# A three-stage transformer step on one core: first transfers and products in another order, causal mask on GpSimd, squares between chunks

## The chip, the cores and the metric

One NeuronCore of a Trainium2 chip runs the kernel. The metric is the device time of one execution in microseconds (us); the other seven cores are not used. "TensorE" is the matrix engine (PE in the rows), "VectorE" DVE, "ScalarE" ACT, "GpSimd" POOL and "SyncE" SP.

## The reference

`x` is 256 rows of 1024 floats. Three layers follow one another, each with residual additions:

1. An even mixer (`moba_nsa_mixer`): RMS norm, one projection into queries, keys, values, gates; eight heads of block attention (with 256 positions there is one block, so plain causal attention with a relative bias) and eight heads with three branches each (compressed, selected, window), whose outputs are weighted by sigmoid gates; then an output projection and an MLP with `relu(h)^2`.
2. An odd mixer (`fox_mixer`): 16 heads of causal attention with a forget bias, then the same kind of MLP.

```
q, k, v, fz = _split(h @ w_in, ODD_SPLITS)
log_f = jax.nn.log_sigmoid((fz + b_forget).astype(jnp.float32))
cum = jnp.cumsum(log_f, axis=1).transpose(0, 2, 1)
s = (einsum('bhqd,bhkd->bhqk', qc, k) * scale + cq[..., None] - cum[:, :, None, :])
p = masked_softmax(s, key_pos[None, :] <= t[:, None])
```

3. A third layer: a gated feed-forward part, a mixer with eight dilated attention heads and four pooling groups, a second gated part, all three with norms modulated by a projection of `c`; a final norm.

All weights and results are float32.

## The kernel before, in words

**Precision and pace.** A float32 product is made of three faster ones of kind float32r: each operand x is split into a rounded part and a remainder, and `three` (L1375 to L1378) adds hi*lo, lo*hi and hi*hi in a PSUM bank. The activations are split when they are made (`a_hi` by ScalarE, `a_lo` by VectorE), the weights when they come in.

**The weight stream.** All large weights come in units of 128x2048 floats (1 MB), in the order in which they are used (`PHASES`), into a ring of four buffers `raw`. SyncE issues the transfer of unit u once TensorE has counted up `unit_used` for unit u-4 (L499 to L508). ScalarE rounds a unit or half a unit to `w_hi` (`round_half` L612, `advance` L623), VectorE subtracts (`rest_half` L937, `advance` L948) and counts up `lo_ready`, for which TensorE waits before the unit's first product. Each of these engines carries out its own list of instructions in order; all waiting is by semaphores.

**The start.** SyncE fetches the first 128 rows of `x`, unit 0 in halves, the other 128 rows, units 1 to 3 and a compression weight; ScalarE's own queue fetches `par`, the table of small constants, in two parts (L811, L812); GpSimd's queue fetches the relative table. ScalarE squares and sums the rows, VectorE makes the inverse root and scales them (`scale`), TensorE transposes them (`turn_rows`, L1457), ScalarE and VectorE split the transposed rows (`turned`, L666 and L1032). TensorE then makes a small product, `rel_rows` (L1612), of the relative table with a selection matrix, from which ScalarE copies `rrow` (L823); GpSimd stores it and reads it back spread over the partitions (`rel_band`), for the relative biases of the heads from the nq1 unit on. Then come units 0 and 1 (`v_even`, values) in eight parts, with the second half's transposes between, and units 2 and 3.

**The mixers.** `plan` lays each mixer out in ticks: a unit has 1, 2 or 4 parts, each a tick. In a tick every engine does what the tick's lists name: scores of a head (TensorE), logits with bias and row minimum (VectorE, L1090), exponential with sum (ScalarE, L751), weighting of the probabilities by the reciprocal sum (GpSimd, `scale` L536), their transposes (TensorE, `turn_probs` L1545) at least 3.8 planned us later, and the product with the values (L1563). `extras` hold what a stage has besides: in the even mixer `kcvc` writes bank 4, from which ScalarE copies the pairs of neighbouring positions (L715, L716), VectorE makes the blocks `blk`, TensorE compresses them (L1635) and goes through `hid30` (L1257), transposes of it (L1647), an exponential, `ck` and `kc` to the compressed scores.

**The forget attention.** Its 16 heads (numbers 24 to 39) take as bias the summed log gates `cum`, stored to DRAM and read back in four transfers of four heads each into `cum_row` (L576), the second to fourth paced by `unit_used`. The causal mask is added by TensorE: one more product per head (L1536) of an identity with the triangle `tri_r` into the two diagonal blocks of the score bank.

**The passages.** Between stages `norm_turn` does for each half t of the rows: residual addition (VectorE), squares with sum (ScalarE, L642), inverse root (both), scaling to `tok`, transposes, splitting. Half 0 is scaled by ScalarE (L682), half 1 by VectorE (L985). In the passage gf1 two norms are fused: VectorE also weighs the squares with a squared gain (`weigh`, L991). TensorE works on in the meantime: the last products of the old stage, then the first of the new that need only half 0 (`begin_hidden`, `begin_values`).

## Time and profile before

| | us |
|---|---|
| median of 3 runs | 1125.08 (1123.85 to 1128.44) |
| profiled execution | 1124.25 |
| its span (first to last instruction) | 1122.4 |
| TensorE busy in it | 1091.3 |
| VectorE busy | 766.7 |
| ScalarE busy | 573.5 |
| GpSimd busy | 98.4 |

The span is what the profiler sees; the time of an execution holds 1.85 us around it. "Busy" counts instructions in work, not waits. TensorE's matmuls overlap, so its busy time is no measure of its efficiency. The times of instructions count from the span's start.

### The profile page before, as it was taken

What the parts mean: (1) busy time and instruction counts of PE and PEld (TensorE: products, weight loads), DVE (VectorE), ACT (ScalarE), POOL (GpSimd) and SP (SyncE); (2) the same over time, 40 slices, a digit from 0 to 9 for tenths busy, and PEclk for the clock granted to TensorE, in tenths of its full rate; (3) what the DMA queues carried; (4) which work ended last, traced back from release to release, by engine and by line L of the source; (5) the groups of instructions that cost most, each with busy time, mean ns of one, the idle gap of its engine ahead of it and who ended that gap; (6) DMA issues with size and microseconds to landing.
All of it is one profiled execution on the core that took longest, in us unless ns stands there. A gap on an engine that the chain in (4) does not pass through costs nothing.

```text
span 1122.4 us, 17638 instructions
## 1 busy us (share of the span) xinstructions
PE 1091.3 (97%) x7206; PEld 979.1 (87%) x7206; DVE 766.7 (68%) x1195; ACT 573.5 (51%) x856; POOL 98.4 (9%) x195
## 2 busy tenths in 40 slices
PE   6999999999999999999999899999999999999997
PEld 5888779999988997899999789999978978999996
DVE  6667677878787775787766777776675766455455
ACT  6666765433356776743433653333355866333333
POOL 1022210101000121100000000101000100000000
PEclk9999999999999999999999999999999999999999
DMA  8752257778864733677778548777644434555551
GB/s 300 290 187 78 76 181 302 273 293 286 290 219 168 260 114 113 244 265 249 263 262 302 196 154 296 265 279 290 215 152 150 151 135 148 186 186 182 186 187 68
DMA packets 39520, 236.82 MB, mean 211 GB/s; under 512 B 4453, under 2 KB 4613, under 8 KB 16528
## 3 DMA queue, kind: packets, MB, share of 16 engines
q1 hardware_dynamic: 26640, 188.76, 46.4%
q0 software_dynamic: 12512, 46.26, 12.1%
q8 instruction: 57, 0.93, 0.3%
q10 hardware_dynamic: 288, 0.68, 0.2%
q14 instruction: 23, 0.19, 0.0%
HBM read 234.58 MB, written 1.10 MB: 210 GB/s over the span
## 4 chain that ended last, share of the span: by engine, by line
PE 88%; DVE 6%; ACT 3%; DMA 2%; issue 1%; SPq 0%; DVEq 0%; ACTq 0%
PE bank L1376 27%; PE bank L1377 26%; PE bank L1378 26%; DMA raw<-in_stream 2%; PE bank L1563 2%; DVE w_lo L937 1%; PE bank L1545 1%; PE bank L1534 1%; ACT w_hi L612 1%; PE bank L1457 1%; PE bank L1533 1%; DVE tok L964 1%; PE bank L1635 1%; DVE h L965 1%; PE bank L1505 0%
## 5 line engine op out<-in xcount | busy, mean ns | idle before, releaser
L1376 PE MATMUL bank<-a_lo,w_hi 128*128 128x256 f32 x1408 | 402.1, 286 | 1.0 <-ACT pair L716 1.0
L1378 PE MATMUL bank<-a_hi,w_hi 128*128 128x256 f32 x1408 | 398.3, 283 | 0.0
L1377 PE MATMUL bank<-a_hi,w_lo 128*128 128x256 f32 x1408 | 398.3, 283 | 0.0
L948 DVE TENSOR_TENSOR w_lo<-raw,w_hi 128x2048 fp32r<-128x2048 f32 x123 | 280.1, 2290 | 146.4 <-ACT w_hi L623 146.3
L623 ACT ACTIVATE w_hi<-raw 128x2048 fp32r<-128x2048 f32 x123 | 235.4, 1917 | 205.6 <-DMA raw<-in_stream 205.6
L1376 PEld LDWEIGHTS bank<-a_lo,w_hi 128*128 128x128 f32 x1408 | 269.7, 192 | 6.6 <-issue 2.6
L1377 PEld LDWEIGHTS bank<-a_hi,w_lo 128*128 128x128 f32 x1408 | 269.8, 192 | 1.8
L1378 PEld LDWEIGHTS bank<-a_hi,w_hi 128*128 128x128 f32 x1408 | 269.7, 192 | 0.0
L1376 PE MATMUL bank<-w_lo,hid_hi 128*128 128x512 f32 x432 | 169.0, 391 | 0.2 <-DVE w_lo L948 0.2
L1377 PE MATMUL bank<-w_hi,hid_lo 128*128 128x512 f32 x432 | 168.6, 390 | 0.0
L1378 PE MATMUL bank<-w_hi,hid_hi 128*128 128x512 f32 x432 | 168.1, 389 | 0.0
L937 DVE TENSOR_TENSOR w_lo<-raw,w_hi 128x1024 fp32r<-128x1024 f32 x102 | 124.5, 1238 | 32.9 <-ACT w_hi L612 32.3
L612 ACT ACTIVATE w_hi<-raw 128x1024 fp32r<-128x1024 f32 x102 | 104.8, 1053 | 29.4 <-DMA raw<-in_stream 29.2
L1378 PEld LDWEIGHTS bank<-w_hi,hid_hi 128*128 128x128 f32 x432 | 81.1, 188 | 17.2
L1376 PEld LDWEIGHTS bank<-w_lo,hid_hi 128*128 128x128 f32 x432 | 81.3, 188 | 16.3 <-issue 0.8
L1377 PEld LDWEIGHTS bank<-w_hi,hid_lo 128*128 128x128 f32 x432 | 81.3, 188 | 14.9
L1152 DVE CUSTOM_DVE_ANT_0 ada_raw<-ada_raw,silu_row 128x1024 f32<-128x1024 f32 x72 | 85.0, 1220 | 0.0
L543 POOL DMA_DIRECT2D ada_raw<-in_ada x72 | 38.1, 529 | 421.4 <-DVE modc L1152 421.4
L1376 PE MATMUL bank<-w_lo,a_hi 128*128 128x512 f32 (+1 forms) x160 | 63.3, 395 | 3.9 <-DVE a_lo L1028 3.3
L536 POOL TENSOR_SCALAR prob<-prob,wgt 128x256 f32<-128x256 f32 x96 | 43.8, 468 | 240.0 <-DVE wgt L1108 181.8
L795 ACT ACTIVATE hid_act<-bank 128x512 f32<-128x512 f32 x28 | 16.7, 596 | 90.6 <-PE bank L1378 90.6
L1378 PE MATMUL bank<-w_hi,a_hi 128*128 128x512 f32 (+1 forms) x160 | 61.7, 385 | 0.0
(203 smaller groups left out, 1159.2 us busy)
## 6 DMA issues: line engine op xcount, KB each, us to landing
raw<-in_stream SPq DMA_DIRECT2D x173, 1024.0 KB, 5.0
ada_raw<-in_ada POOLq DMA_DIRECT2D x72, 512.0 KB, 6.5
cmpw<-in_stream SPq DMA_DIRECT2D x4, 1024.0 KB, 8.2
rel_band<-rel_scratch POOLq DMA_DIRECT2D x2, 1024.0 KB, 10.3
cum_row<-cum_scratch POOLq DMA_DIRECT2D x4, 512.0 KB, 7.7
h<-in_x SPq DMA_DIRECT2D x2, 512.0 KB, 6.6
raw<-in_stream SPq DMA_DIRECT2D x2, 512.0 KB, 7.8
silu_row<-in_c_row POOLq DMA_DIRECT2D x2, 512.0 KB, 4.3
```

The lines of the kernel that those rows point to most:

```text
L536: ins = pool.tensor_scalar(p_, p_, wgt[:, 2 * i + t:2 * i + t + 1], 1.0, ALU.mult, ALU.mult)
L543: pool.dma_start(ada_raw[:, p % ADA_BUFS, :], ada[p]).then_inc(ada_landed[p % ADA_BUFS], 16)
L612: nc.scalar.activation(w_hi[:, u % RING, part_], raw[:, u % RING, part_], ACT.Copy).then_inc(hi_ready, 1)
L623: nc.scalar.activation(w_hi[:, u % RING, :], raw[:, u % RING, :], ACT.Copy).then_inc(hi_ready, 2)
L795: nc.scalar.activation(hid_act[:, j % 3, :], ps[MLP_BANKS[j % 3]][:, :], ACT.Relu).then_inc(act_feat, 1)
L937: nc.vector.tensor_tensor(w_lo[:, u % RING, part_], raw[:, u % RING, part_], w_hi[:, u % RING, part_].bitcast(F32), ALU.subtract).then_inc ...
L948: nc.vector.tensor_tensor(w_lo[:, u % RING, :], raw[:, u % RING, :], w_hi[:, u % RING, :].bitcast(F32), ALU.subtract).then_inc(lo_ready, 2)
L1152: nc.vector.tensor_tensor_reduce(part, part, silu_row[:, :], 1.0, 0.0, ALU.mult, ALU.add, modc[:, p:p + 1]).then_inc(ada_done, 1)
L1376: nc.tensor.matmul(dst, l_hi, r_lo, start=start, stop=False)
L1377: nc.tensor.matmul(dst, l_lo, r_hi, start=False, stop=False)
L1378: return nc.tensor.matmul(dst, l_hi, r_hi, start=False, stop=stop)
L1563: ins = nc.tensor.matmul(ps[ob][HD * half:HD * half + HD, c0 + block * P:c0 + T], v_cols(kind, block, heads[j][3], HD), probT[:, j % 4, lo ...
```

## The change

- **First transfers.** The second, larger part of `par` is fetched by SyncE behind unit 3 and no longer by ScalarE's queue at the start.
- **Products of zeros.** VectorE clears a tile first of all, and TensorE multiplies it 20 times by itself (`WARM`), 128x128 each in float32, before the first transposes.
- **The rel product** moves from ahead of units 0 and 1 to behind them, from bank 6 to bank 4; the transposes no longer wait for its inputs, and ScalarE copies `rrow` after it has split the second half's transposed rows, but still ahead of units 2 and 3. TensorE's wait for the copy moves to the `kcvc` unit.
- **Even mixer.** `nq0` is computed in bank 7 instead of 4, so its wait for the pairs goes to `qm0`. The transposes of `hid30` for the keys, the exponential behind them and `ck`/`kc` each come one tick later.
- **Causal mask.** TensorE's mask products, `ident_r`, `tri_r` and the semaphore for them go. GpSimd adds the triangle instead: for each of the four chunks of four heads one addition of 128x512 into a new tile `cum_early` (rows of half 0) and one into `cum_row` (half 1, diagonal block), each behind the chunk's landing and in GpSimd's own queue ahead of the weighting; VectorE waits for `masked` where it waited for the landing.
- **Passages.** In all six, ScalarE takes the squares of half 1 between the chunks of half 0 and scales half 1 too; VectorE no longer scales, and does its unit's remainder after the inverse root of half 1 instead of before.

```diff
@@ GpSimd
+            def mask(c):
+
+                pool.wait_ge(cum_landed[c], 16)
+                four = slice(4 * c, 4 * c + 4)
+                tri = pc_("tri", P).unsqueeze(1).to_broadcast([P, 4, P])
+                pool.tensor_tensor(cum_early[:, four, :], cum_row[:, four, 0:P], tri, ALU.add).then_inc(masked, 1)
+                pool.tensor_tensor(cum_row[:, four, P:T], cum_row[:, four, P:T], tri, ALU.add).then_inc(masked, 1)
...
-            for c in range(4):
+            pool.wait_ge(par_landed, 16)
+            for c in range(5):
+                if c < 4:
+                    if c > 0:
+                        pool.wait_ge(unit_used, FIRST["qk_fox"] + c - 1)
+                    pool.dma_start(cum_row[:, 4 * c:4 * c + 4, :], ...).then_inc(cum_landed[c], 16)
                 if c > 0:
-                    pool.wait_ge(unit_used, FIRST["qk_fox"] + c - 1)
-                pool.dma_start(cum_row[:, 4 * c:4 * c + 4, :], ...).then_inc(cum_landed[c], 16)
+                    mask(c - 1)
             scale(*FOX)
@@ SyncE
                 sp.dma_start(raw[:, u % RING, :], stream[u]).then_inc(raw_landed[u % RING], 16)
+                if u == RING - 1:
+                    sp.dma_start(par[:, COLS["pool_scale"]:N_COLS], cols[:, COLS["pool_scale"]:N_COLS]).then_inc(par_landed, 16)
@@ ScalarE
             def norm_turn(name, gain, shift=None):
 
-                for t in range(TT):
-                    squares(name, t)
-                    if t == 0:
-                        round_half()
-                        scale(name)
-                    turned(name, t, gain, shift)
-                    if t == 0:
-                        round_half()
+                squares(name, 0)
+                round_half()
+                scale(name, 0)
+                turned(name, 0, gain, shift, (0, 1))
+                square_half(name, 1, 0)
+                turned(name, 0, gain, shift, (2, 3))
+                square_half(name, 1, 1)
+                round_half()
+                root(name, 1)
+                scale(name, 1)
+                turned(name, 1, gain, shift)
...
-            act.dma_start(par[:, COLS["pool_scale"]:N_COLS], cols[:, COLS["pool_scale"]:N_COLS]).then_inc(par_landed, 16)
...
             squares("mix0", 1)
             round_half()
+            turned("mix0", 1, pc_("mix0", KT))
             act.wait_ge(rel_rows, 1)
-            nc.scalar.activation(rrow[:, :], ps[6][0:16, 0:REL], ACT.Copy).then_inc(rel_rows_sb, 1)
-            turned("mix0", 1, pc_("mix0", KT))
+            nc.scalar.activation(rrow[:, :], ps[4][0:16, 0:REL], ACT.Copy).then_inc(rel_rows_sb, 1)
             act.wait_ge(par_landed, 16)
             advance(FIRST["v_even"] + 4)
@@ VectorE
                 turned(name, 0, gain, shift, (2, 3))
-                rest_half()
...
                 else:
                     inverse_root(name, 1)
-                scale(name, 1)
+                rest_half()
                 turned(name, 1, gain, shift)
...
+            nc.vector.memset(probT[:, 0, 0:P], 0.0).then_inc(zeros_set, 1)
...
-            nc.vector.tensor_copy(ident_r[:, :], ident)
-            nc.vector.tensor_copy(tri_r[:, :], pc_("tri", P)).then_inc(const_ready, 1)
...
-                        dve.wait_ge(cum_landed[c], 16)
+                        dve.wait_ge(masked, 2 * c + 2)
@@ TensorE
-                if name == "mix0":
-                    pe.wait_ge(rel_rows_sb, 1)
...
-                if kind == "fox":
-                    ins = nc.tensor.matmul(bank[:, P:3 * P], ident_r[:, :], tri_r[:, :].unsqueeze(1).to_broadcast([P, 2, P]),
-                                           start=False, stop=True)
...
+            pe.wait_ge(zeros_set, 1)
+            for _n in range(WARM):
+                nc.tensor.matmul(ps[0][:, 0:P], probT[:, 0, 0:P], probT[:, 0, 0:P], start=True, stop=True)
+            pe.wait_ge(norms_landed, 16)
+            turn_rows("mix0", 0)
+            begin_values("mix0", lambda j, part: value_part("mix0", "v_even", j, part, 4, V1W))
             pe.wait_ge(pick_landed, 32)
             pe.wait_ge(pool_step, 1)
-            pe.wait_ge(norms_landed, 16)
-            turn_rows("mix0", 0)
-            nc.tensor.matmul(ps[6][0:16, 0:REL], relt[:, :], rpick[:, :], start=True, stop=True).then_inc(rel_rows, 1)
-            begin_values("mix0", lambda j, part: value_part("mix0", "v_even", j, part, 4, V1W))
+            nc.tensor.matmul(ps[4][0:16, 0:REL], relt[:, :], rpick[:, :], start=True, stop=True).then_inc(rel_rows, 1)
             pe.wait_ge(par_landed, 16)
...
-                for v, where in enumerate((("nq1", 0, 3), ("km0", 0, 1))):
+                for v, where in enumerate((("qm0", 0, 0), ("km0", 0, 1))):
...
-                if tick.at("qm0", 0, 2):
+                if tick.at("qm0", 0, 3):
...
                 elif tag == "kcvc":
+                    if part == 0:
+                        pe.wait_ge(rel_rows_sb, 1)
                     feature_part(u, 4, part, 2)
...
-                    if tag == "nq0" and part == 0:
+                    if tag == "qm0" and part == 0:
                         pe.wait_ge(pairs_taken, 2)
```

## Rows read from the trace of the kernel before

**Rows 1.** The page, busy time and share of the span of each engine.
```profile
PE 1091.3 (97%) x7206; PEld 979.1 (87%) x7206; DVE 766.7 (68%) x1195; ACT 573.5 (51%) x856; POOL 98.4 (9%) x195
```

**Rows 2.** TensorE's waits: us in total, times, longest.
```profile
PE bank L1457 <- DMA rpick<-in_rel_pick: 8.9, 1, 8.9
PE bank L1457 <- DVE tok L985: 5.8, 6, 2.5
PE bank L1376 <- ACT pair L716: 1.0, 1, 1.0
PE bank L1647 <- DVE hid L1257: 0.9, 1, 0.9
```

**Rows 3.** TensorE in order of time: start, us, what, idle before.
```profile
10.81 1.89 PE L1612 MATMUL bank<-rpick,relt 33*16 33x511 f32 x2
12.92 0.79 PE L1376 MATMUL bank<-w_lo,a_hi 128*128 128x512 f32 x1 [0.23 <-DVE a_lo L1032]
17.05 0.50 PE L1376 MATMUL bank<-w_lo,a_hi 128*128 128x512 f32 x1
18.22 1.04 PE L1457 MATMUL bank<-par,tok 128*128 128x128 f32 x8
19.50 0.50 PE L1376 MATMUL bank<-w_lo,a_hi 128*128 128x512 f32 x1 [0.24 <-DVE w_lo L937]
25.16 0.47 PE L1376 MATMUL bank<-w_lo,a_hi 128*128 128x512 f32 x1
```

**Rows 4.** ScalarE in order of time, the start.
```profile
10.03 1.06 ACT L612 ACTIVATE w_hi<-raw 128x1024 fp32r<-128x1024 f32 x1 [0.45 <-DMA raw<-in_stream]
17.41 0.57 ACT L823 ACTIVATE rrow<-bank 16x511 f32<-16x511 f32 x1
20.65 3.77 ACT L623 ACTIVATE w_hi<-raw 128x2048 fp32r<-128x2048 f32 x2
```

**Rows 5.** VectorE in order of time, the start.
```profile
11.12 1.22 DVE L937 TENSOR_TENSOR w_lo<-raw,w_hi 128x1024 fp32r<-128x1024 f32 x1 [0.28 <-ACT w_hi L612]
22.72 4.49 DVE L948 TENSOR_TENSOR w_lo<-raw,w_hi 128x2048 fp32r<-128x2048 f32 x2 [0.94 <-ACT w_hi L623]
```

**Rows 6.** The chain of waits, at two places: start, us, what.
```profile
654.51 1.78 PE bank L1505 x16
378.32 0.17 PE bank L1536
385.38 0.33 PE bank L1545 x3
```

**Rows 7.** GpSimd: one line, landings of cum_row, and its order of time.
```profile
L583 POOL TENSOR_TENSOR gate_row<-row x1: 2522/2522/2522, 467.0 to 467.0; 128x1024 f32<-128x1024 f32 x1
DMA to landing us min/median/max: 7.1/7.7/8.7
363.45 1.06 POOL L576 DMA_DIRECT2D cum_row<-cum_scratch  x2 [1.85 <-DMA cum_scratch<-cum]
375.32 0.53 POOL L576 DMA_DIRECT2D cum_row<-cum_scratch  x1 [5.23 <-PE bank L1378]
382.01 0.83 POOL L536 TENSOR_SCALAR prob<-prob,wgt 128x256 f32<-128x256 f32 x2 [6.17 <-DVE wgt L1108]
386.53 1.87 POOL L536 TENSOR_SCALAR prob<-prob,wgt 128x256 f32<-128x256 f32 x2 [3.69 <-DVE wgt L1108]
```

**Rows 8.** DMA issues of the first 60 us: KB, us to landing.
```profile
par<-in_cols ACTq DMA_DIRECT2D x1, 567.0 KB, 7.9
```

**Rows 9.** One stretch: busy us of engines, granted clock, DMA share, GB/s.
```profile
10.00:15.00 5.00, 4.77 (x13) 2.39 (x12) 4.25 (x11) 4.32 (x11) 0.00 (x0) 1.00 1.03 425
```

**Rows 10.** The scaling of rows on VectorE and ScalarE: ns min/median/max.
```profile
L985 DVE TENSOR_SCALAR tok<-h,stat x14: 478/483/489, 7.6 to 928.9; 128x512 f32<-128x512 f32 x14
L682 ACT ACTIVATE tok<-h,stat x10: 707/716/725, 150.7 to 920.2; 128x512 f32<-128x512 f32 x10
```

**Rows 11.** TensorE in order of time, passage gf1.
```profile
646.25 1.09 PE L1457 MATMUL bank<-par,tok 128*128 128x128 f32 x8 [2.51 <-DVE tok L985]
```

More of the change, by code:

```diff
@@ L45 @@
 ADA_BUFS = 3
+WARM = 20
 PHASES = [
@@ L239, in build @@
         cum_row = place("cum_row", [P, 16, T], at=bias_at)
+        cum_early = place("cum_early", [P, 16, P], at=V_at + 2 * D * 4)
         dil_b = place("dil_b", [P, HEADS, T], at=bias_at)
@@ L258, in build @@
         par = place("par", [P, N_COLS])
-        ident_r = place("ident_r", [P, P], F32R)
-        tri_r = place("tri_r", [P, P], F32R)
         kc = place("kc", [P, 2, 2, 16], F32R)
@@ L624, in advance, with square_half @@
                     halves[0] += 2
+            def square_half(name, t, k):
+                n = NORMS.index(name)
+                if name == "mix0":
+                    act.wait_ge(x_landed[t], 16)
+                else:
+                    act.wait_ge(h_ready, 4 * (n - 1) + 2 * t + k + 1)
+                half = slice(512 * k, 512 * k + 512)
+                accum = fin[:, t, k:k + 1] if name == "gf1" else stat[:, k, t:t + 1]
+                nc.scalar.activation(tok[:, t, half], h[:, t, half], ACT.Square, scale=1.0 / 32, accum_out=accum).then_inc(sumsq, 1)
             def squares(name, t):
-                sums_of_squares(name, t)
-                root(name, t)
-            def sums_of_squares(name, t):
-                n = NORMS.index(name)
                 if t == 0:
                     nc.scalar.activation(stat[:, 10, :], stat[:, 9, :], ACT.Sqrt)
-                for k in range(2):
-                    if name == "mix0":
-                        act.wait_ge(x_landed[t], 16)
-                    else:
-                        act.wait_ge(h_ready, 4 * (n - 1) + 2 * t + k + 1)
-                    half = slice(512 * k, 512 * k + 512)
-                    accum = fin[:, t, k:k + 1] if name == "gf1" else stat[:, k, t:t + 1]
-                    nc.scalar.activation(tok[:, t, half], h[:, t, half], ACT.Square, scale=1.0 / 32, accum_out=accum).then_inc(sumsq, 1)
+                square_half(name, t, 0)
+                square_half(name, t, 1)
+                root(name, t)
             def root(name, t):
@@ L649, in root, with turned @@
                     nc.scalar.activation(fin[:, t, 10:12], fin[:, t, 4:6], ACT.Sqrt).then_inc(root_ready, 1)
-            def turned(name, t, gain, shift=None):
+            def turned(name, t, gain, shift=None, chunks=(0, 1, 2, 3)):
                 m = TURN[name] + 4 * t
                 ts = slice(t * P, (t + 1) * P)
-                for c in range(4):
+                for c in chunks:
                     if shift is not None and c % 2:
@@ L840, in even_extras @@
                         nc.scalar.activation(hid_e[:, v, :], ps[(2, 7)[v]][HD:HD + 30, 0:256], ACT.Copy).then_inc(hidden_half, 1)
-                for v, where in enumerate((("qm0", 0, 0), ("km0", 0, 2))):
+                for v, where in enumerate((("qm0", 0, 1), ("km0", 0, 2))):
                     if tick.at(*where):
@@ L1257, in even_extras @@
                         nc.vector.tensor_tensor(hid30[:, v, :], ps[(2, 7)[v]][0:30, 0:256], hid_e[:, v, :], ALU.add).then_inc(hidden_rows, 1)
-                for v, where in enumerate((("qm0", 0, 0), ("km0", 0, 2))):
+                for v, where in enumerate((("qm0", 0, 1), ("km0", 0, 2))):
                     if tick.at(*where):
@@ L1628, in compress @@
             def compress(v, half):
+                if v == 1:
+                    pe.wait_ge(feat_taken, 2 * STACK_NO[("nq0", 0)] + 2)
                 pe.wait_ge(blocks_ready, v + 1)
```

34 lines of the change are left out of this document (16 added, 18 removed).

## The prediction

> **What bounds the kernel now.** I read the busy times first: TensorE is busy for 1091.3 of the 1122.4 us of the span [rows 1], so only what shortens TensorE's own work, or its idle 31 us, can move the end. Next come TensorE's waits [rows 2]: 8.9 us at the start for the last small transfer, 5.8 us in six passages between stages, where the second half's transposes wait for VectorE's scaled rows, 1.0 us for ScalarE's pair copies and 0.9 us for VectorE's hid30. Then I read the start in order of time on TensorE, ScalarE and VectorE [rows 3 to 5] and the stretch of the forget attention [rows 6, 7]. The profiled execution took 1124.25 us, 1.85 us more than its span, and 0.83 us less than the median of 1125.08. I add up against 1124.25 and put the 0.83 back at the end. About 0.5% (5.6 us) is what a measurement can tell here from no change.
>
> **First transfers.** The 567 KB of `par` leave the ScalarE queue, where they moved beside the first units for 7.9 us [rows 8], and go behind unit 3 on SyncE's. The transfers ran at 425 GB/s in that stretch with all the engines' share used [rows 9], so 567 KB less ahead is 1.3 to 1.6 us. Who gets it: ScalarE's second rounding at 10.03 waited for its transfer [rows 4], VectorE's remainder at 11.12 waited for ScalarE [rows 5], and TensorE's first product at 12.92 for VectorE [rows 3]. The same chain sets the product at 19.50, which waited for w_lo. Bounds: 0 (the small queue was served in gaps) to 1.6; I take 1.4, since 567 KB lie fully ahead of unit 1. SyncE issues one more transfer (0.4 us) while it has nothing due, and the compression weights behind it are used only some units later.
>
> **Zeros ahead.** 20 products of 128x128 start at about 0.9 us. Eight of the same form take 1.78 us [rows 6], 0.22 each, so twice that at half speed: they end between 5.3 and 9.8 us; the first transposes stood at 8.9 [rows 2]. What they buy is the clock. The 12 products from 12.92 take 4.13 us; the 6 after them 1.17 (17.05 to 18.22) [rows 3]. By these spacings the first ran at 1.2 GHz and the next at 2.4 GHz, although the table's granted clock says 1.00 [rows 9]. But the time saved, 1.8 us, lies ahead of waits that others set: product 19.50 waits for w_lo, whose chain runs through transfers, ScalarE and VectorE. So it is worth 0; bounds 0 to -0.3, and +0.5 if all zeros run slow.
>
> **The rel product.** Before, this product (1.89 us, at half speed) ran at 10.81 and ended when TensorE had to wait anyway; its copy by ScalarE (0.57) ran at 17.41, before ScalarE rounded units 2 and 3 (3.77 for both, at 20.65); VectorE's remainders (4.49 for both) began at 22.72, and unit 2's products at 25.16 just met them [rows 3 to 5]. Now the product stands behind the eight parts of units 0 and 1, and ScalarE waits for it before the copy and before any rounding of unit 2. Behind that wait are queued the copy, unit 2's rounding, then on VectorE its remainder, and TensorE waits for that. From the end of unit 1's products: product at full speed 0.95, semaphore and drain 0.2, copy 0.57, rounding 1.92, remainder 2.25, two hand-overs 0.1: 6.0 us, where the gap was 0.2. Unit 2 starts 5.8 later and, with the 1.4 from the transfers, 4.4 later: at 29.5 instead of 25.16. **Term: +4.4**, bounds +4.2 (transfers give 1.6) to +5.8 (they give nothing). TensorE stands idle for 5.0 of it.
>
> **What the mixer gives back.** The 1.0 us wait for the pairs [rows 2] came from ScalarE, held up by a late transfer; the compression behind it waited 0.2 us more for blk, made of the same pairs. With TensorE 4.4 us later and the first product of the nq0 unit moved to bank 7, neither is left: -1.2. hid30's transposes move one tick later (a quarter of a unit; units 2 and 3 are the stretch from 25.16 on, some 4.4 us each), more than the 0.85 us that was waited: -0.85. The chain behind them (exponential, keys, `kc`) keeps one tick of slack less; I cost that at 0, and at +1 if VectorE's `kc` is late at km0. Bounds of the two: 0 to -3.5 (all the waits of this stage). **Term: -2.05.**
>
> **Mask on GpSimd.** 16 products `tri_r x ident_r` go, each 0.17 us of the chain [rows 6]: -2.7 (bounds -2.2 to -2.7). GpSimd gets 8 additions of 128x512. The nearest row, its product of 128x1024, took 2.52 [rows 7]: 1.26 each, 2.5 per chunk. These masks stand in one queue with the transfers and with the weighting of the probabilities. In order: transfer 0, issued at 363.45, lands 7.7 later, about 371.2; mask 0 to 373.7; only then is transfer 2 issued, mask 1 to 376.8; then transfer 3 is issued (was 375.32) and lands at 384.5; mask 3 to 387.0; then head 24's weighting (0.8, before at 382.01) to 387.9. Its transposes stood at 385.38 [rows 6], 384.9 without the three mask products ahead of it. That is a new wait of 3.0 us. One more thing: at 386.53 two weightings took 1.87, at 382.01 two had taken 0.83; VectorE was subtracting two SBUF tiles meanwhile [rows 7]. Half of such a block gives 0.5 more. **Term: -2.7 + 3.5 = +0.8**, bounds -1.2 (landing 7.1 each, additions at 1.0) to +8.
>
> The Trainium skill ("SBUF — State Buffer", "Who interferes with whom") says that a VectorE instruction with two SBUF inputs and a GpSimd instruction that reads SBUF exclude each other for their whole length. The row of 1.87 agrees; the rule speaks against this edit, and its price is rival D.
>
> **Passages.** The second half's scaling moves to ScalarE: 0.716 per half where VectorE took 0.483 [rows 10]. VectorE's remainder (1.2) now comes behind the inverse root, but ScalarE's rounding (1.04) comes between the second square and the root. In the five plain and gated passages this cancels: first scaled half earlier by 0.2, second half as before, -0.1 each. In gf1 TensorE waited 2.5 us, until 646.25 [rows 11]; VectorE weighs both halves of the row there behind its remainder (1.2), which now comes after the roots; about 0.7 of it is left once ScalarE's later squares are taken off. **Term: -1.2**, bounds +1 (six roots held up by a late transfer behind the rounding) to -5.8 (every wait for `tok` gone).
>
> **Sum.** 4.4 - 2.05 + 0.8 - 1.2 = +1.95: 1126.2 for the profiled execution, 1127.0 beside the median.
>
> **Rivals.**
> B, the clock falls in the new 5.0 us wait. For: TensorE began at half speed after 8.9 idle microseconds [rows 2, 3]. Against: after the longest later wait, 2.5 us ahead of 646.25 [rows 11], eight transposes took 1.09, as at full speed (1.04 at 18.22 [rows 3]). 5.0 lies between, nearer the 2.5. The price is that of a start at half speed, 1.8: 1128.8. The Trainium skill ("TensorE: Matmul & The Clock Gate", "Why this matters for your kernels") asks to leave no long idle gaps between bursts, because the clock halves after one; by it B would be the likelier.
> C, the passages close. The squares taken between chunks bring all six waits for `tok` to nothing: 5.8 in place of 1.2, so 1122.4. For: VectorE loses three instructions of the chain; against: ScalarE has them in it, longer. With the even stage at its bound (-3.5) as well: 1121.
> D, slower: the masks line up. Place: GpSimd's queue ahead of head 24. If every addition is held by one of VectorE's remainders (1.2 us), a chunk takes 4.9: mask 0 ends at 376.1, mask 1 at 381.5, transfer 3 lands at 389.2, mask 3 ends at 394.2, the weighting at 395.9. The wait is 11.0 instead of 3.5: 1134.5. Three chunks stand in that chain, so from 3.7 us a chunk on the time passes 1130.7. Against: the row of 1.87 is two weightings of which at most one was held.
>
> **Numbers.** Forecast 0.42, B 0.24, C 0.19, D 0.10, others 0.05. The likeliest gives 1127.0. The range takes in B and the most of C and ends inside D: 1121.5 to 1132.5. Faster by over 0.5% (under 1119.5) needs C with every other bound: 0.11. Slower by over 0.5% (over 1130.7) is D and the tail of B: 0.16. Within: 0.73.
>
> **What would show it.** TensorE idle for some 5 us before unit 2's first product near 29.5, released by w_lo; ScalarE's rel copy just behind the rel product; that product at about 0.95. Zeros ending before 9, products at 12 at 0.23 apart. No mask products; a wait of about 3 us before head 24's transposes, released by GpSimd; mask additions of 1.26. Passage waits near 0.5 each (1.8 in gf1), released by ScalarE's `tok`. It is wrong if unit 2 starts before 27, if that wait for GpSimd is missing, or if the passage waits vanish.

## The result: 0.2 to 0.3% slower

| | before | changed |
|---|---|---|
| median, us | 1125.08 (5 runs, 1123.85 to 1128.44) | 1129.31 (5 runs, 1126.27 to 1132.6) |
| the same kernel timed once more beside the kernel before | 1125.6 (23 runs) | 1127.48 (12 runs, 1125.56 to 1132.19) |
| profiled execution, us | 1124.25 | 1126.27 |
| its span, us | 1122.4 | 1124.5 |

The ratio, changed over before, is 1.0032 with a 95% interval of [1.0017, 1.0048] in the first measurement and 1.0021 [1.001, 1.0033] in the second. Both intervals lie above 1, so the small loss is clear of the noise of the runs. All 17 executions together have their median at 1127.95. The forecast was 1126.2 for the profiled execution (measured 1126.27) and 1127.0 for the median.

The profile after. First the page's busy row, beside [rows 1]: TensorE is busy 5.8 us more although 2.7 us of mask products are gone, because the zeros ahead count 7.1 and the products at half speed, further down, count longer.
```profile
PE 1097.1 (98%) x7230; PEld 983.6 (87%) x7230; DVE 764.7 (68%) x1182; ACT 580.9 (52%) x868; POOL 108.6 (10%) x203
```
TensorE's waits after (total us, times, longest), beside [rows 2]: the first line is new; the second stands where VectorE's `tok` had 5.8.
```profile
PE bank L1391 <- DVE w_lo L965: 5.0, 1, 5.0
PE bank L1472 <- ACT tok L697: 4.0, 6, 1.8
PE bank L1391 <- DVE a_lo L1049: 2.5, 1, 2.5
PE bank L1544 <- DVE low L1106: 1.8, 3, 1.0
```
TensorE after, in order of time (start, us, what, idle before), beside [rows 3].
```profile
1.05 7.12 PE L1619 MATMUL bank<-probT 128*128 128x128 f32 x40 [1.05 <-DVE probT L1229]
11.73 0.50 PE L1391 MATMUL bank<-w_lo,a_hi 128*128 128x512 f32 x1 [2.48 <-DVE a_lo L1049]
12.91 0.62 PE L1391 MATMUL bank<-w_lo,a_hi 128*128 128x512 f32 x1
18.32 0.50 PE L1391 MATMUL bank<-w_lo,a_hi 128*128 128x512 f32 x1 [0.43 <-DVE w_lo L954]
23.93 1.03 PE L1625 MATMUL bank<-rpick,relt 33*16 33x511 f32 x2
29.95 0.76 PE L1391 MATMUL bank<-w_lo,a_hi 128*128 128x512 f32 x1 [4.99 <-DVE w_lo L965]
```
ScalarE and VectorE after, the same stretch, beside [rows 4, 5]. Read it as a chain: the rel product ends, ScalarE leaves a wait of 5.55 us for the copy, rounds unit 2, and VectorE leaves a wait of 7.17 us for its remainder.
```profile
24.99 0.59 ACT L841 ACTIVATE rrow<-bank 16x511 f32<-16x511 f32 x1 [5.55 <-PE bank L1625]
25.49 3.69 ACT L638 ACTIVATE w_hi<-raw 128x2048 fp32r<-128x2048 f32 x2
27.51 4.49 DVE L965 TENSOR_TENSOR w_lo<-raw,w_hi 128x2048 fp32r<-128x2048 f32 x2 [7.17 <-ACT w_hi L638]
```
Four stretches after (busy us per engine, then the granted clock, DMA share, GB/s), the first beside [rows 9]. In the last two the granted clock is 0.66.
```profile
10.00:15.00 5.00, 3.27 (x12) 2.61 (x12) 4.52 (x11) 4.25 (x13) 0.00 (x0) 0.79 1.02 424
15.00:20.00 5.00, 4.57 (x24) 3.79 (x24) 4.59 (x16) 3.33 (x10) 0.00 (x0) 0.87 1.01 414
25.00:30.00 5.00, 0.05 (x1) 0.08 (x1) 2.49 (x2) 5.00 (x4) 0.49 (x1) 0.66 0.98 374
30.00:35.00 5.00, 5.00 (x19) 4.28 (x20) 5.00 (x4) 2.97 (x4) 0.00 (x0) 0.66 0.34 143
```
GpSimd and VectorE after, in the forget attention, beside [rows 7]. An addition of 128x512 takes 1.10 us alone; the one of 379.83 and the one before it (1.51) are held up, and so is VectorE's remainder at 382.41: 3.26 us where 1.22 is usual, beside two additions of 1.10 and 1.09 that run undisturbed from 382.42.
```profile
375.66 1.10 POOL L547 TENSOR_TENSOR cum_early<-cum_row,par 128x512 f32<-128x512 f32 x1 [6.96 <-DMA cum_row<-cum_scratch]
379.83 2.07 POOL L548 TENSOR_TENSOR cum_row<-cum_row,par 128x512 f32<-128x512 f32 x1
382.42 1.10 POOL L547 TENSOR_TENSOR cum_early<-cum_row,par 128x512 f32<-128x512 f32 x1
387.48 1.09 POOL L547 TENSOR_TENSOR cum_early<-cum_row,par 128x512 f32<-128x512 f32 x1 [2.90 <-DMA cum_row<-cum_scratch]
389.60 0.83 POOL L539 TENSOR_SCALAR prob<-prob,wgt 128x256 f32<-128x256 f32 x2
382.41 3.26 DVE L954 TENSOR_TENSOR w_lo<-raw,w_hi 128x1024 fp32r<-128x1024 f32 x1
```

**Where the time went.** The transposes of the second half of the rows in each passage, and two places ahead of them, are landmarks in both traces. How much later each comes after:

| place | before | after | later by |
|---|---|---|---|
| unit 2's first product | 25.16 | 29.95 | +4.79 |
| first transposes behind the even mixer | 151.75 | 155.94 | +4.19 |
| second half of that passage | 158.82 | 162.53 | +3.71 |
| second half, into the forget attention | 341.88 | 345.90 | +4.02 |
| second half, out of it | 460.21 | 463.14 | +2.93 |
| gf1 | 646.25 | 648.59 | +2.34 |
| last passage | 929.08 | 931.14 | +2.06 |

So the start lost 4.8, and everything behind it gave back 2.7 (4.79 - 2.06).

### The profile page after: what moved, and what is told of

Same layout as the page of the kernel before. It is cut to its first block, busy times and chain, and to the rows that moved or that the text cites. A ratio compares the mean times of both kernels' runs of the same rounds, so it can differ in the third digit from the quotient of the medians.

```text
span 1124.5 us, 17693 instructions
## 1 busy us (share of the span) xinstructions
PE 1097.1 (98%) x7230; PEld 983.6 (87%) x7230; DVE 764.7 (68%) x1182; ACT 580.9 (52%) x868; POOL 108.6 (10%) x203
## 4 chain that ended last, share of the span: by engine, by line
PE 89%; DVE 5%; ACT 4%; DMA 2%; issue 1%; SPq 0%; DVEq 0%; ACTq 0%
PE bank L1391 27%; PE bank L1392 27%; PE bank L1393 27%; PE bank L1571 2%; DMA raw<-in_stream 2%; PE bank L1553 1%; PE bank L1545 1%; ACT tok L649 1%; ACT w_hi L627 1%; PE bank L1472 1%; PE bank L1544 1%; DVE w_lo L954 1%; DVE h L982 1%; DVE tok L981 1%; PE bank L1649 1%
## 5 line engine op out<-in xcount | busy, mean ns | idle before, releaser
L954 DVE TENSOR_TENSOR w_lo<-raw,w_hi 128x1024 fp32r<-128x1024 f32 x102 | 128.1, 1275 | 28.2 <-ACT w_hi L627 27.8
L1392 PE MATMUL bank<-w_hi,a_lo 128*128 128x512 f32 (+1 forms) x160 | 62.1, 388 | 0.0
```

Of the source, the lines that this page charges most:

```text
L954: nc.vector.tensor_tensor(w_lo[:, u % RING, part_], raw[:, u % RING, part_], w_hi[:, u % RING, part_].bitcast(F32), ALU.subtract).then_inc ...
L1392: nc.tensor.matmul(dst, l_lo, r_hi, start=False, stop=False)
```

## The experiments

Each kernel is the changed one with the edit shown, except where it says otherwise. "Copy late" means the edit of the first. Lines left out of a diff are marked `...`. Each ratio is against the kernel before on the same chip, and its 95% interval reaches 1.0 to 1.7 us either way, so a difference of under 1 us between two experiments is no finding. Medians of the kernel before, on the same chips, were 1124.82 (first four), 1125.59 (next four), 1125.6 (next three) and 1125.26 (the last). Diffs name code, not lines; ScalarE is `act` or `nc.scalar`.

**1. The copy behind ScalarE's rounding of units 2 and 3.**
```
+            act.wait_ge(par_landed, 16)
+            advance(FIRST["v_even"] + 4)
             act.wait_ge(rel_rows, 1)
             nc.scalar.activation(rrow[:, :], ps[4][0:16, 0:REL], ACT.Copy).then_inc(rel_rows_sb, 1)
-            act.wait_ge(par_landed, 16)
-            advance(FIRST["v_even"] + 4)
```


> The changed kernel with one thing moved: ScalarE copies rrow behind the rounding of units 2 and 3 and not ahead of it. Theory 1 (ScalarE's wait for the rel product is what holds unit 2, and the clock falls in that wait): TensorE's wait of 5.0 us ahead of unit 2 shrinks to under 0.3, unit 2 starts near 25.0 instead of 29.95, its products come 0.23 us apart from the first; of the 6.7 us that are gained there, up to 1.5 come back because nq0 and the compression meet a ScalarE that is less ahead. Span 1124.5 - 5.0 - 1.7 + 0 to 1.5: 1117.8 to 1119.3, some 4 to 6 us under the kernel before. Rival (the stream of units sets the time there, so the wait only moves): unit 2 starts near 25, but TensorE waits 3 us or more for units 3 to 6 and the span stays above 1122.

Measured: 1122.15, ratio 0.9975 [0.996, 0.999]; profiled 1119.89, span 1118.1. Its rows, ScalarE first and then TensorE's unit 2, and the granted clock of that stretch:
```profile
19.11 3.77 ACT L638 ACTIVATE w_hi<-raw 128x2048 fp32r<-128x2048 f32 x2
24.83 0.59 ACT L843 ACTIVATE rrow<-bank 16x511 f32<-16x511 f32 x1 [1.95 <-PE bank L1625]
24.72 0.50 PE L1391 MATMUL bank<-w_lo,a_hi 128*128 128x512 f32 x1
```
```profile
30.00:35.00 5.00, 5.00 (x35) 4.61 (x34) 2.43 (x3) 2.01 (x2) 0.95 (x1) 1.00 0.99 300
```
Unit 2 starts 5.23 us sooner and the clock doesn't fall. The span is 6.4 us shorter: 5.2 for the wait and, with it, the 1.7 of the clock. Of these 6.9 the even mixer gives 1.3 back (the first passage comes 5.66 sooner, and TensorE now waits 1.08 for `blk` at 49.10), and 0.7 more is gained on the way to the forget attention. Moving this one instruction in ScalarE's list takes away more than the whole loss: the span is 4.3 us under that of the kernel before.

**2. Products of zeros in the 5.0 us wait,** so that the clock is kept and the wait is not.
```
             nc.tensor.matmul(ps[4][0:16, 0:REL], relt[:, :], rpick[:, :], start=True, stop=True).then_inc(rel_rows, 1)
+            pe.wait_ge(act_split, TURN["mix0"] + 8)
+            for _n in range(20):
+                nc.tensor.matmul(ps[5][:, 0:P], probT[:, 0, 0:P], probT[:, 0, 0:P], start=True, stop=True)
```


> The changed kernel with 20 more products of zeros (4.4 us at full speed) behind the rel product, inside the 5.0 us wait for unit 2's remainder: the wait stays, TensorE works in it. Theory 1: the clock's fall costs 1.7 us of its own; unit 2 starts at 29.95 as before but at 0.23 us a product, so unit 3 and all that follows comes 1.7 us earlier, span 1122.8; and as the fall is a matter of chance in length, the median of the runs falls more (some 3 us) and they lie closer together. Rival (half speed there is hidden by what ScalarE and VectorE do at the same time): the products are fast, but the first compression stands at 54.8 as before and the span stays at 1124.5.

Measured: 1129.23, ratio 1.0033 [1.002, 1.0046], no better than the changed kernel's median; profiled 1123.54, span 1121.7. In the profiled execution the clock is kept:
```profile
30.00:35.00 5.00, 5.00 (x30) 4.41 (x29) 5.00 (x5) 2.50 (x3) 0.36 (x1) 1.00 0.17 71
```
Its unit 2 starts 0.47 us sooner than in the changed kernel's first trace and its first passage comes 2.06 sooner (153.88 against 155.94), which leaves 1.6 us as the clock's price; 0.7 more, on the way to the forget attention, makes up the 2.8 us less span. But the spans of its 12 executions go from 1121.7 to 1129.8, and the median shows nothing of the 1.6. The idea that this wait's clock makes the executions spread fell here, and what its longer executions lose is open, since only the shortest was profiled: the executions of 1121.7 and 1127.4 have the same mean granted clock, 0.996, and that of 1129.8 has 0.995.

**3. Only the rel product and its copy moved,** in the kernel before.
```
-            act.wait_ge(rel_rows, 1)
-            nc.scalar.activation(rrow[:, :], ps[6][0:16, 0:REL], ACT.Copy).then_inc(rel_rows_sb, 1)
             turned("mix0", 1, pc_("mix0", KT))
+            act.wait_ge(rel_rows, 1)
+            nc.scalar.activation(rrow[:, :], ps[4][0:16, 0:REL], ACT.Copy).then_inc(rel_rows_sb, 1)
...
-            nc.tensor.matmul(ps[6][0:16, 0:REL], relt[:, :], rpick[:, :], start=True, stop=True).then_inc(rel_rows, 1)
             begin_values("mix0", lambda j, part: value_part("mix0", "v_even", j, part, 4, V1W))
...
+            nc.tensor.matmul(ps[4][0:16, 0:REL], relt[:, :], rpick[:, :], start=True, stop=True).then_inc(rel_rows, 1)
```


> The kernel before with one part of the change alone: the rel product and its copy behind units 0 and 1 (bank 4, waits as in the changed kernel). Theory 1: unit 2 starts 5.9 us later (31.1), at half speed for 3 us (1.7 more); 1 to 2 us come back at nq0. Span 1122.4 + 5.9 + 1.7 - 1.5 = 1128.5, times 5 to 7 us above the kernel before. Rival (the step is worth no more than its product): 1 us above.

Measured: 1131.92, ratio 1.006 [1.0047, 1.0073]; span 1129.4. TensorE at unit 2, and the clock behind it:
```profile
31.11 0.76 PE L1376 MATMUL bank<-w_lo,a_hi 128*128 128x512 f32 x1 [4.96 <-DVE w_lo L948]
```
```profile
30.00:35.00 5.00, 3.89 (x13) 3.34 (x14) 5.00 (x4) 4.16 (x5) 0.00 (x0) 0.53 0.59 241
```
The move alone brings the wait and the fall: unit 2 comes 5.95 us later than before, 31.11 against 25.16. In the full change it comes 1.16 sooner than here, at 29.95: that is what the first transfers give (ScalarE's second rounding starts 1.20 sooner, at 8.84 against 10.04).

**4. The mask on TensorE again.**
```
-                pool.tensor_tensor(cum_early[:, four, :], cum_row[:, four, 0:P], tri, ALU.add).then_inc(masked, 1)
-                pool.tensor_tensor(cum_row[:, four, P:T], cum_row[:, four, P:T], tri, ALU.add).then_inc(masked, 1)
...
+                if kind == "fox":
+                    ins = nc.tensor.matmul(bank[:, P:3 * P], ident_r[:, :], tri_r[:, :].unsqueeze(1).to_broadcast([P, 2, P]),
+                                           start=False, stop=True)
```


> The changed kernel with the causal mask back on TensorE (the 16 mask products, no additions on GpSimd). From the traces, the stretch from the passage mix1 to the passage mlp1 gave the changed kernel 0.9 us net: 2.7 for the products less 1.0 of a wait for a logit and 0.8 elsewhere. Theory 1 (the additions hold VectorE's remainders, 4.05 and 3.26 us for work of 2.36 and 1.22, not GpSimd's weighting): without them VectorE's remainders take 1.22 again, the 1.0 us wait is gone, and the span is 0.6 to 1.0 longer: 1125.3. Rival (the additions cost more than they save, as GpSimd's queue was predicted to): shorter than 1124.5.

Measured: 1127.3, ratio 1.0022 [1.0013, 1.0031]; span 1124.2, spans of ten executions 1124.2 to 1127.4. The forget attention takes 118.02 us where the changed kernel's first trace has 117.24, yet the median is no longer than the changed kernel's (1127.95 over its 17 executions). The saving that the first trace shows doesn't reach the median.

**5. Copy late, and the passages as before** (squares of a half together, VectorE scales half 1, its remainder ahead of the inverse root).
```
-                turned(name, 0, gain, shift, (0, 1))
-                square_half(name, 1, 0)
-                turned(name, 0, gain, shift, (2, 3))
-                square_half(name, 1, 1)
+                turned(name, 0, gain, shift)
                 round_half()
-                root(name, 1)
-                scale(name, 1)
+                squares(name, 1)
...
```


> The kernel with the late copy (the copy of rrow behind the rounding of units 2 and 3), and the passages as before: half 1 squared in one go and scaled by VectorE, remainder ahead of the inverse root. In the traces the six passages gave 0.48, 0.2, 0.35, 0.8, 0.15 and 0.15, 2.1 us in all. Theory 1: span 1118.1 + 2.1 = 1120.2, waits for tok again 5.8 in six. Rival (the passages' gain as predicted, 1.2, the rest was given by other edits): 1119.3.

Measured: 1125.21, ratio 0.999 [0.998, 1.0001]. That is 3.1 us above experiment 1; TensorE's waits for `tok` are 6.5 us again, and behind the 2.51 us of gf1 its clock fell in this execution (0.66 from 645 to 650). In the traces 2.9 us of the difference already stand ahead of the first passage (153.21 against 150.28: a wait of 2.58 for `blk` where experiment 1 has 1.08, and a fall of the clock at 86 us). So the pair doesn't price the passages. Experiments 9 and 10 do.

**6. Copy late, and the mask on TensorE.**

> The kernel with the late copy and the causal mask back on TensorE. By the traces so far the mask on GpSimd is worth 0.8 us in an execution like the profiled one: span 1118.9. Theory 2 (GpSimd's queue is what makes the executions with masks lie further apart, 1118.7 to 1126.6, and their middle above the profiled one: in some of them transfers and additions line up and head 24 or the remainders wait longer): the runs lie within 3.5 us and the median is 1120.5 to 1121.5, under the 1122.15 with masks on GpSimd, although the profiled span is longer. Rival (the spread comes from the start, from the length of the clock's low stretches): spread and median as with masks on GpSimd, 1122.5 to 1123.

Measured: 1120.68, ratio 0.9958 [0.9946, 0.997]; spans 1118.3 to 1120.3, where those of experiment 1 go from 1116.8 to 1124.8. In its trace the clock falls nowhere before the end. The shortest executions of experiment 1 are shorter, its median is 1.5 longer. So the expectation that came true is the one on GpSimd's masks: they save in some executions and cost in others. The spread rests on 5 executions here.

**7. Copy late, `WARM = 0`** (no zeros ahead).

> The kernel with the late copy and no product of zeros (WARM 0). Theory 1: the zeros are worth nothing on the path, because the product at 18.15 waits for w_lo either way; the first products come at half speed until about 16 to 17, and the span stays at 1118.1 within 0.3. Rival (the zeros save what a start at half speed costs): 1 to 1.8 us longer.

Measured: 1119.81, ratio 0.9949 [0.9936, 0.9962]; profiled 1121.7. The product that waits for unit 1's second half starts at 18.23, with the zeros at 18.32: they buy nothing. What this trace showed besides was not expected by either theory, the wait that the prediction had asked for:
```profile
384.42 0.90 PE L1553 MATMUL bank<-par,prob 128*128 128x128 f32 x3 [2.19 <-POOL prob L539]
```

**8. The rel product and its copy in their old places,** all else as changed.
```
             turn_rows("mix0", 0)
+            nc.tensor.matmul(ps[6][0:16, 0:REL], relt[:, :], rpick[:, :], start=True, stop=True).then_inc(rel_rows, 1)
             begin_values("mix0", lambda j, part: value_part("mix0", "v_even", j, part, 4, V1W))
...
-            nc.tensor.matmul(ps[4][0:16, 0:REL], relt[:, :], rpick[:, :], start=True, stop=True).then_inc(rel_rows, 1)
```


> The changed kernel with the rel product and its copy where the kernel before had them (bank 6, behind the first transposes, copy ahead of the second half's splitting); all else as changed. Theory 1: the product (1.0 to 1.9 us) lies in the 2.4 us in which TensorE waits for the first a_lo, the copy in ScalarE's 0.9 us ahead of bank_turned, both free; span 1118.1 - 1.0 = 1117.1, 5 us under the kernel before. Rival (product and copy delay the first splitting): 1118 or more, no better than the late copy.

Measured: 1121.28, ratio 0.9964 [0.995, 0.9978]; span 1120.8, where 1117.1 was expected. Unit 2 starts at 23.77 without a wait. The 3.7 us over the expectation hold a wait of 1.83 us for GpSimd at head 24, one of 1.33 for `blk` and a fall of the clock at 85 us (0.66).

**9. As 8, with the mask on TensorE.**

> The changed kernel with the rel product and its copy in their old places and the causal mask added by TensorE again; the transfers, the zeros and the passages as changed. Theory (the order of the copy cost the time; the masks on GpSimd spread the executions): the unit-2 wait stays under 0.6 us, the stretch of the forget attention is within 0.3 us of 118.0, the median is 1.5 us below that of the same kernel with masks on GpSimd (1121.28), so 1119.8, and the spans lie within 2.5 us of one another. Rival (masks are worth nothing either way, the spread is the chip's): 1121.3, spread 4 us or more.

Measured: 1120.89, ratio 0.9959 [0.9946, 0.9972]; spans 1118.4 to 1121.0. The stretch of the forget attention is 118.05. The median is 0.4 below that of 8, between the theory's 1.5 and the rival's nothing, and too small for runs on two chips to tell from nothing. The wait ahead of unit 2 is 0.48, as the theory asked (under 0.6).

**10. As 9, with the passages of before.**

> As the run before it (rel product and copy in their old places, mask on TensorE) with the passages back too: squares of half 1 together, its scaling on VectorE, its inverse root behind its remainder. Only the order of the first transfers, the zeros, the bank of nq0 and the tick of hid30 are left of the change. Theory (the passages are worth 2.1 us on their own, as the trace's landmarks show): 2.1 us slower than the run before it, so 1121.9; the waits for the rows `tok` near 6.5 us in place of 4. Rival (the passages gain only together with a faster or slower neighbour, such as GpSimd's masks): within 0.7 us of the run before it. Against the kernel before, what is left is worth 1.4 (transfers) + 2.05 (the even mixer's waits): 1121.6 by the prediction's terms.

Measured: 1123.03, ratio 0.9978 [0.997, 0.9987]. 2.14 us above 9, as the theory said, and the two intervals just touch: the gain is there, its size is known to some 1.7 us either way. In the traces the distances between the transposes of the two halves shrink by 2.3 us over the six passages, but the spans are only 0.9 apart, because in the trace of 9 TensorE waited 0.99 us for the first half's `tok` in gf1, and its clock fell behind the next wait. TensorE's transposes of gf1 here, and (in the second fence) in the kernel of experiment 12, which has the new passages and no wait ahead of the first half:
```profile
644.46 1.14 PE L1460 MATMUL bank<-par,tok 128*128 128x128 f32 x8 [2.51 <-DVE tok L987]
```
```profile
643.77 1.27 PE L1463 MATMUL bank<-par,tok 128*128 128x128 f32 x8 [1.65 <-ACT tok L686]
```

**11. The changed kernel once more,** to see where a longer execution loses.

> The changed kernel itself, once more, to see which stretch a slower execution loses in. Theory (two things vary: how long the clock stays at half speed behind the 5.0 us wait, and whether GpSimd holds up head 24): the wait before unit 2 is 5.0 again and its products up to 33 us run at half speed; if this execution's span is above 1126.5, the stretch of the forget attention is over 118.2 us (117.2 in the first profile) with a wait for GpSimd at head 24, or the first compression comes after 55.3 us (54.81). Rival (the variation is spread over the whole span): all landmarks drift evenly, no stretch over 0.5 us longer than in the first profile. Median 1129.3 by both.

Measured: 1127.48, as in the table at the top; this profiled execution has a span of 1129.0, 4.5 more than the first. Its chain of waits in the forget attention (start, us, what) reads as the prediction wrote it: transfer, two masks, issue, two masks, transfer, two masks, weighting, and only then TensorE.
```profile
368.82 7.84 DMA cum_row<-cum_scratch
376.74 1.10 POOL cum_early L547
377.84 1.06 POOL cum_row L548
378.90 0.52 POOL cum_row L589
379.44 1.50 POOL cum_early L547
380.94 1.99 POOL cum_row L548
382.92 5.22 DMA cum_row<-cum_scratch
388.20 1.10 POOL cum_early L547
389.30 1.05 POOL cum_row L548
390.36 1.79 POOL prob L539 x2
```
And TensorE in order of time: behind each of these waits the products soon stand 0.21 us apart (0.43 for those of 512 columns) in place of 0.12 (0.23). The windows show the granted clock.
```profile
392.19 0.55 PE L1553 MATMUL bank<-par,prob 128*128 128x128 f32 x3 [1.75 <-POOL prob L539]
393.49 0.41 PE L1392 MATMUL bank<-a_hi,w_lo 128*128 128x256 f32 x1
393.70 0.41 PE L1393 MATMUL bank<-a_hi,w_hi 128*128 128x256 f32 x1
651.72 1.44 PE L1472 MATMUL bank<-par,tok 128*128 128x128 f32 x8 [1.75 <-ACT tok L697]
653.38 0.63 PE L1392 MATMUL bank<-w_hi,a_lo 128*128 128x512 f32 x1
```
```profile
393.00:398.00 5.00, 5.00 (x32) 5.00 (x32) 0.99 (x5) 1.98 (x7) 1.81 (x4) 0.66 0.00 0
650.00:655.00 5.00, 3.28 (x13) 2.69 (x14) 4.10 (x13) 3.99 (x10) 0.00 (x0) 0.77 0.00 0
```
By the landmarks the 4.5 us are 1.4 ahead of the first passage (unit 2 starts 0.39 sooner, but its products stay at half speed until 34.9 and not 33.4, and a wait of 0.80 for ScalarE at 75.27 is new), 1.9 in the forget attention (119.17 against 117.24, most of it the GpSimd wait and the clock behind it) and 1.4 between gf1 and the next passage (194.72 against 193.29, the clock alone: that wait is 1.75 in both). The other stretches agree within 0.15. The rival, an even drift, is out for this execution.

**12. Copy late, mask on TensorE, no zeros.**

> The changed kernel with ScalarE's copy behind its rounding of units 2 and 3, the causal mask added by TensorE again, and no zeros ahead: the transfers and the passages are all that is left of the change, beside the place of the rel product. Theory (the zeros are worth nothing, and the medians below differ by which executions hit a fall of the clock): as the same kernel with the zeros, 1120.7, spans from 1118 to 1121, unit 2's wait gone and the stretch of the forget attention within 0.3 us of 118.0. Rival (the zeros cost time, as the medians of the pair with masks on GpSimd, 1122.15 with and 1119.81 without, could be read): 1118.4.

Measured: 1121.64, ratio 0.9964 [0.9952, 0.9976]; spans 1118.1 to 1120.3. With the zeros, on another chip, it was 1120.68: the zeros' worth can't be told from nothing. The reading of the pair 1 and 7 as a price of the zeros (2.3 us) fell.

**The masks, over all traces.** From the second transposes into the forget attention to those out of it, in us:

| mask on | passages | one value for each profiled execution |
|---|---|---|
| TensorE | before | 118.33, 118.31, 118.34 |
| TensorE | changed | 118.02, 118.03, 118.05, 118.03 |
| GpSimd | before | 116.78 |
| GpSimd | changed | 117.24, 117.22, 117.32, 118.29, 119.62, 119.17 |

The mean of the last line is 118.14, 0.1 above that of the second. GpSimd's masks turn a fixed 118.0 into anything from 0.8 less to 1.6 more. The longest and the shortest span of a kernel lie 3.4 to 8.1 us apart in the changed kernel and its variants with the mask on GpSimd (5 to 12 executions each), and 2.0 to 3.2 in the variants with it on TensorE (5 to 11 each). The kernel before, with its mask on TensorE, shows 2.7 to 4.5 over 10 to 27 executions, so part of the spread has other causes.

**The best version** is not one: experiments 6, 7, 8, 9 and 12 are all between 1119.8 and 1121.7 with intervals that overlap, 0.4 to 0.5% below the kernel before. The steadiest are those with the mask on TensorE (6, 9 and 12).

## Why the prediction was right, and where it was not

**First transfers: right.** ScalarE's second rounding starts at 8.84 (10.03 before), the product that waits for `w_lo` at 18.32 (19.50). That is 1.2 where 1.4 was taken; experiment 3 gives 1.16.

**Zeros: right at 0,** though not for all the reasons given. They end at 8.17, just ahead of the transposes, which then take 1.07 in place of 1.97. The first products do run at full speed (11.73), but from 12.91 on at half, as the granted clock of 0.79 says. The value chain behind is set by transfers, as argued. Experiments 7 and 12 take the zeros away at no cost that shows. The 0 holds for the changed kernel's trace, not for every execution: in that of experiment 9 the products stayed at half speed until 17.6, the second transposes came at 17.74 (16.73 in experiment 8) and unit 2 0.9 later.

**The rel product: right, the main step.** Unit 2 at 29.95 (forecast 29.5) after 4.99 us idle (5.0), released by `w_lo`; the rel product in 1.03 (0.95). The term was +4.4, measured +4.79: 0.2 from the transfers, 0.2 from the product and the hand-overs. Experiments 1, 3 and 8 show the cause from both sides: the wait goes when the copy or the product is put back, and comes when the pair alone is moved.

**What the mixer gives back: right.** The waits for pairs, blk and hid30 are gone from the trace. They are gone because TensorE comes late: with the copy late, or in its old place, a wait for `blk` of 0.3 to 2.6 us is there again in all eight traces. From unit 2 to the first passage the changed kernel takes 125.99 us, before 126.59, with 1.7 of lost clock in it: 2.3 given back, forecast 2.05.

**The clock (rival B, 0.24): it happened, and I had it as the less likely.** The forecast put this term at nothing; it was +1.7. In the trace the nine products from 29.95 to 33.34 take 3.39 us, twice their time at full speed. I argued from one row, the 2.5 us wait of gf1 after which the transposes ran fast [rows 11]. That row was one draw. After the same 2.51 us wait the clock fell in the traces of experiments 5 and 10 and not in that of 3; in experiment 11 it fell after 1.75, twice. Behind the 5.0 us wait it fell in all four traces that left TensorE idle in it (the changed kernel's two, experiments 3 and 4). The Trainium skill ("TensorE: Matmul & The Clock Gate", "Why this matters for your kernels") warns of long idle gaps between bursts; the traces agree for the 5.0 us wait, and the falls behind 1.75 and 2.51 us came after shorter waits than that section warns of. A single unharmed gap was no argument against it.

**Mask: mis-sized, and it is what kept the sum right.** The term was -2.7 + 3.5 = +0.8. In the first trace it was -1.1 (118.33 to 117.24, of which 0.3 belongs to the passages). The wait of 3.0 us for GpSimd wasn't there, which the prediction itself had named as a sign of being wrong: each undisturbed addition took 1.10 instead of 1.26, and transfer 3, issued at 381.84, had landed by 387.48, after 5.6 us and not 7.7. VectorE bore the conflict instead: its 3.26 us remainder left TensorE waiting 1.0 us for a logit. GpSimd's weighting ended at 390.43 and head 24's transposes started at 390.48, so by these rows a wait for GpSimd of about that 1.0 would have stood there instead. Either way the conflict costs about 1 us here.

In three other traces (experiments 7, 8 and 11) the forecast wait did come, with 2.19, 1.83 and 1.75 us. There the weighting ahead of it took 1.8 to 1.9 us in place of 0.83: one of VectorE's remainders ran at that moment (in the first trace none did), and it cost more than the 0.5 that the prediction added. So the queue is a real path, and its price changes from one execution to the next, around 2 us and not 3.5. The rule cited for it (the Trainium skill, "SBUF — State Buffer", "Who interferes with whom") holds in both directions here: now GpSimd's addition is the one held (2.07), now VectorE's remainder (3.26, close to the two additions beside it and its own 1.22). The kernel before had shown this price next to the row that priced the additions: beside GpSimd's 2.52 us product at 467 [rows 7] two remainders, 2.4 us alone, took 4.05 from 466.60. Rival D's wait of 11 us was seen in no trace.

**Passages: right in sign, too small.** Term -1.2, measured -2.14 in the medians of experiments 9 and 10; in the profiled execution some -1.4 is left (-0.5, +0.3, -0.3, -0.6 and -0.3 in the sum below). I had called the five plain ones a draw, -0.1 each. In the first three the whole wait of some 0.58 closed, which the prediction had named, for all six, as a sign of being wrong (in the first, the distance of the two halves' transposes goes from 7.07 to 6.59); gf1's wait fell by 0.75, to 1.76, as forecast, and the last two stages' transposes came 0.13 closer each. What failed is the step "in the five plain and gated passages this cancels". Counted from the first half's transposes of the first passage, ScalarE's square root started at 5.46 before and at 4.75 in experiment 9: the squares taken between the chunks ended 0.86 sooner, and VectorE's mean no longer stood behind its remainder. The first scaled half of the rows was ready 0.5 sooner (forecast 0.2), the second 0.3 sooner (forecast 0).

**The sum.** Forecast +1.95 for the profiled execution, measured +2.0: +4.8 start, +1.7 clock, -2.3 mixer, -0.5 and +0.3 to the next passage, -1.1 forget attention, -0.6 gf1, -0.3 the last two. A clock term left out (+1.7) met a mask term 1.6 too high (+0.8 against -0.8 with the passages' 0.3 taken off). The right sum is in part luck: two errors of 1.6 to 1.7 us with opposite signs.

**The median.** It lies 1 to 3 us above the profiled execution because that one was the shortest of its five and the third shortest of all 17; I had assumed that the 0.83 of before would carry over. Against the kernel before it is 4.2 us more in the first measurement and 1.9 in the second; the forecast was 1.9, so the first, with 5 executions, lay high. The profile of experiment 11 shows what a longer execution has more of: stretches at half speed behind waits of about 2 us (1.4 us at gf1) and the wait for GpSimd. The granted clock agrees: of the 17 executions the three longest (spans 1129.0, 1130.4, 1130.8) have a mean of 0.990, the five under 1125 have 0.993 to 0.996. It isn't all of it, as experiment 2 shows.

## What to carry to other kernels

When a small instruction moves in one engine's list, look at what stands behind it in that list: here a 0.6 us copy that waits for a late product held back 1.9 us of rounding, 2.3 us of remainders and TensorE. Price a wait of some 2 us or more on TensorE as the wait plus a chance of a further 0.9 to 1.7 us at half speed (0.9 in the forget attention of experiment 11 beside that of 8, 1.4 at gf1, 1.7 at unit 2). And before work is given to GpSimd beside VectorE, expect the saving to come back as spread: test it over many executions, since one trace can show either side.

## What the hardware showed that I had not expected

- Behind the 5.0 us wait the granted clock fell in all four traces. After shorter waits it fell in some traces and not in others with the same wait: after 2.51 us in two of four; after the waits of 1.63 to 1.76 us in gf1 in one of nine; after the waits for GpSimd of 2.19 and 1.75 and not after that of 1.83; not after 2.58 for `blk` (experiment 5). In experiment 9 it fell in gf1 behind two waits of 0.99 and 1.49 us, some 1.5 us of work between them; the second of them stands in all traces and did no harm in the others. What decides it stays open.
- In three traces the granted clock fell in the even mixer as well, with no wait at all, directly behind the 16 products of 128x32 of the compressed scores, which take 1.96 us (0.66 at 85 to 90 us in experiments 5 and 8; 0.77 at 90 to 95 in experiment 3). In experiment 1 the same products left it at full speed.
- Zeros ahead did not keep the clock safely. In the traces of experiments 6, 8 and 10 the granted clock from 10 to 15 us is 1.00 and the value products ran at full speed; in the changed kernel's two and in those of experiments 1, 2, 4, 5 and 9 it is 0.58 to 0.79, and they went to half speed within the stretch. The wait just ahead of the products is 1.5 to 2.0 us in the first three and 1.4 to 2.5 in the others.
- One of GpSimd's 128x512 additions took 1.10 us alone and 1.5 to 2.1 against VectorE; VectorE's 1.22 us remainder took up to 3.27 in return.
